# A four-layer network in float32 on one core: VectorE takes over two of eight weight subtractions in nine stages, and the ring of raw weight tiles goes from four slots to eight

## The chip, the core and the metric

The kernel runs on one core of one Trainium2 chip. The metric is device time in microseconds of one execution, median over runs. A core has TensorE (PE: matrix products into PSUM), VectorE (DVE), ScalarE (ACT), GpSimd (POOL) and SyncE (SP, which here issues the loads of the weights); each works through its own list of instructions in order and waits on semaphores for the others.

## The reference

One sequence of 256 tokens and 2048 channels runs through four layers: a gated linear attention with a linear recurrent unit, an mLSTM, a latent attention with a block attention, and a windowed attention with a dilated one, each with its norm, its gates, its input and output products. Nearly all of the arithmetic is in products of 256 tokens with float32 weight matrices. Cut down to the shape of one layer (the last):

```python
def odd_layer(x, mem, norm_g, w_in, sinks, mem_norm_g, w_mem_kv, w_out):
    h = rms_norm(x, norm_g) @ w_in
    qkv_c, qkv_d, q_mem, gate = split_cols(h, ODD_SPLITS)
    ...
    y = jnp.concatenate([o_c, o_d, o_m], axis=-1) * jax.nn.silu(gate)
    return x + (y @ w_out).astype(x.dtype)
```

## The kernel before

**Stages.** The weight products are 26 stages in a fixed order (`stage_table`): ein, ein_zx, ein_zb, ple0, eout, gate0, oqk, ogate, ov, ogz, ple1, oout, gate1, evc, evkpe, evmem, uq, ukv, evgate_a, evmoba, evgate_b, evout, odin, odmem, odgate, odout. A stage computes pairs: a pair is 2 output blocks of 128 channels by 256 tokens, and it is cut along the contraction into units, 8 for 16 blocks of the contraction and 10 for the 20 blocks of evout and the 18 of odout. A unit is a weight tile of 128 x 512 (four cells of 128 x 128; in odout the last two units of a pair have two cells). There are 1420 units in all, and every one is loaded once.

**A unit's way.** Float32 products are made of parts of fewer bits. For unit n: SP loads `raw` by DMA; ACT rounds it to `w_hi` (in `rounded`, line 738); POOL subtracts, `w_lo = raw - w_hi` (line 340); PE does three matmuls for each cell, `w_hi` with both halves of x and `w_lo` with the high half (lines 381 to 383). `raw`, `w_hi` and `w_lo` each have SLOTS = 4 slots. The waits between them are counts of units:

```python
sp.wait_ge(lo_ready, unit - SLOTS + 1)     # SP: load n after subtraction n - 4
act.wait_ge(unit_used, unit - SLOTS + 1)   # ACT: round n after PE used n - 4
pool.wait_ge(act_rounded, unit + 1)        # POOL: subtract n after rounding n
pe.wait_ge(lo_ready, st.unit0 + p * st.upp + q + 1)   # PE: use n after subtraction n
```

**What else the engines do.** DVE takes each finished pair out of PSUM (`take`, line 1217; in the output stages `hp + sums`, lines 1516 and 1837) and between two pairs does the work of the stage around: it splits activations into high and low halves (`split`, lines 1203 to 1207), adds squares for the next norm (`add_squares`, line 1257), multiplies h by the last gain (`gained`, line 1831), computes inverse roots (`root`, `inverse`, lines 1247 and 1270 to 1281) and rotates keys and queries (lines 1702 to 1705). In evout and odout (`add_out`) its body for pair p begins with the squares of pair p - 1:

```python
if not (isinstance(p, int) and p < 2):
    add(p - 1)                       # waits for ACT's square of pair p - 1
tt(hp, hp, sums_of(st, p, par), ADD).then_inc(pair_out, 1)
```

and ACT issues that square (line 777) right behind the rounding of unit 8 of pair p (`out_norm`, `q == 8`). In odin, pairs 0 to 5 also split a piece of the memory input (`memory`) behind `take`. PSUM banks alternate, so PE may be up to two pairs ahead of DVE.

`pairs_loop` makes two pairs one trip of a hardware loop where there are at least two trips.

Of the kernel before, what the change touches and what calls it, by code (L numbers as in the profile page):

```python
# [80 lines left out]

def stages():
# [26 lines left out]
def build(nc, A, out):  # L109
# [12 lines left out]
    with ctx:  # L122
# [58 lines left out]
        cols_loaded, consts_loaded = sem("cols_loaded"), sem("consts_loaded")  # L181
        unit_loaded = [sem(f"unit_loaded{i}") for i in range(SLOTS)]
        act_rounded, lo_ready, unit_used = sem("act_rounded"), sem("lo_ready"), sem("unit_used")
        pair_out = sem("pair_out")
# [84 lines left out]

        def pairs_loop(eng, count, body, first=0, steps=None, per=0):  # L270

            trips = (count - first) // 2
            if trips >= 2:
                n0 = steps.n if steps else 0
                with eng.Fori(0, trips) as i:  # L275
                    for k in range(2):
                        if steps:
                            steps.n = n0 + i * (2 * per) + k * per
                        body(i * 2 + (first + k), (first + k) % 2)
                if steps:  # L280
                    steps.n = n0 + trips * 2 * per
                first += 2 * trips
            for p in range(first, count):
                body(p, p % 2)

# [4 lines left out]
        def square_sums(name):  # L290
# [3 lines left out]
            return {"x2": (w[:, 40:42, :], 1), "ckv": (sq_next, 1)}.get(name, (sq_sum, 0))  # L294

        def unit_of(st, p, par, q):

            turn, slot = divmod(par * st.upp + q, SLOTS)
            loads = (p - par) * (st.upp * 16 // SLOTS) + (st.unit0 // SLOTS + turn + 1) * 16
            return slot, st.sizes[q], st.unit0 + p * st.upp + q, loads  # L300

# [3 lines left out]
        @block.sync  # L305
        def _(sp):
            def load(st):
                wd = A["w_" + st.name]

                def pair(p, par):  # L310
                    at = 0
                    for q in range(st.upp):
                        slot, n, unit, _ = unit_of(st, p, par, q)
# [7 lines left out]
                if st.unit0 == 0:  # L321
                    pair(0, 0)
                pairs_loop(sp, st.pairs, pair, first=int(st.unit0 == 0))

            for name in [r[0] for r in stage_table()]:
                load(ST[name])
            for k in range(4):
                sp.wait_ge(h_ready, HR["last"] + k + 1)
                sp.dma_start(out[:, 4 * k:4 * k + 4, :], h[:, 4 * k:4 * k + 4, :]).then_inc(out_stored, 16)
            sp.wait_ge(out_stored, 64)  # L330


        @block.gpsimd
        def _(pool):
            def split(st):
                def pair(p, par):
                    for q in range(st.upp):
                        slot, n, unit, _ = unit_of(st, p, par, q)
                        pool.wait_ge(act_rounded, unit + 1)  # L339
                        nc.gpsimd.tensor_tensor(w_lo[:, slot, 0:n], raw[:, slot, 0:n],  # L340
                                                w_hi[:, slot, 0:n].bitcast(F32), SUB).then_inc(lo_ready, 1)

                pairs_loop(pool, st.pairs, pair)

            for name in [r[0] for r in stage_table()]:
                split(ST[name])
# [3 lines left out]
        def _(pe):  # L350
            mm = nc.tensor.matmul

            def product(st, p, par, new=None, units=None):
# [9 lines left out]
                for q in units:  # L363
                    cells, slot = st.units[q], (par * st.upp + q) % SLOTS
# [21 lines left out]
            def products(name, first=0, count=None, new=None, behind=None, peel=1):  # L386


                st = ST[name]
                count = st.pairs if count is None else count  # L390

                def pair(p, par):
                    product(st, p, par, new if isinstance(p, int) and p == 0 else None)
                    if behind:
                        behind(p, par)

                for p in range(first, first + peel):
                    pair(p, p % 2)
                pairs_loop(pe, count, pair, first + peel)

# [312 lines left out]
        def _(act):  # L713
# [18 lines left out]
            def rounded(st, p, q, par=None):  # L732

                slot, n, unit, loads = unit_of(st, p, p % 2 if par is None else par, q)
                act.wait_ge(unit_loaded[slot], loads)
                if not (isinstance(p, int) and unit < SLOTS):
                    act.wait_ge(unit_used, unit - SLOTS + 1)
                af(w_hi[:, slot, 0:n], raw[:, slot, 0:n], ACT.Copy).then_inc(act_rounded, 1)  # L738

            def stage(name, first=0, count=None, peel=1, behind=None, done=0):  # L740
# [12 lines left out]
                for p in range(first, first + peel):  # L753
                    pair(p, p % 2)
                pairs_loop(act, count, pair, first + peel)

# [438 lines left out]
        def _(dve):  # L1195
# [4 lines left out]
            def split(src, gain, x, kt, count):  # L1200
# [7 lines left out]
                dve.wait_ge(x_ready, count)  # L1208

            def sums_of(st, p, par):  # L1210
# [8 lines left out]
            def store(name, buf, at, scale, first=0, count=None, adding=None, behind=0):  # L1219
# [10 lines left out]
                pairs_loop(dve, st.pairs if count is None else count, pair, first)  # L1230
                dve.wait_ge(pair_out, STORED[name] + (st.pairs if count is None else count))

# [97 lines left out]
            step(tt(col("ev_norm"), col("ev_norm"), col("final_norm"), MUL))  # L1330
            store("ein", w, 0, RS_LAYER, 3, 10, adding="mem", behind=2)
            store("ein", w, 0, RS_LAYER, 10, 11)
# [175 lines left out]
            def tail(l, x_out, x_h, x_next, gain_next, x_next_buf):  # L1508

                st = ST[f"ple{l}"]  # L1510
                pairs_loop(dve, 8, lambda p, par: take_plain(st, p, par), 4)
                so, xo = ST["eout" if l == 0 else "oout"], X[ST[f"gate{l}"].x]

                def out_pair(p, par):
                    hp = h[:, ds(p * 2, 2), :]
                    tt(hp, hp, sums_of(so, p, par), ADD).then_inc(pair_out, 1)  # L1516
                    dve.wait_ge(pair_out, so.pair0 + p + 1)
# [281 lines left out]
            def results_pair(name, rope_at, kind, nb, memory_behind=False):  # L1799
# [19 lines left out]
            def add_out(name, x_next, gain):  # L1819
# [13 lines left out]
                def pair(p, par):  # L1833
                    if not (isinstance(p, int) and p < 2):
                        add(p - 1)
                    hp = h[:, ds(p * 2, 2), :]
                    tt(hp, hp, sums_of(st, p, par), ADD).then_inc(pair_out, 1)  # L1837
# [10 lines left out]
                pairs_loop(dve, 8, pair, 2, steps=step, per=2 if x_next else 1)  # L1848
                add(7)
# [232 lines left out]
```

## Time and profile before

| | us |
|---|---|
| runs, median of 3 (lowest to highest) | 2476.62 (2474.54 to 2477.72) |
| the profiled execution | 2478.6 |
| its span, first to last instruction | 2476.8 |
| PE busy (share of the span) | 2290.4 (92%) |
| POOL busy | 1944.8 (79%) |
| DVE busy | 1319.7 (53%) |
| ACT busy | 1188.2 (48%) |

An instruction row gives start, length, engine, line, operation and tiles, and in brackets the idle time of the engine before it with what ended that. Matmul rows overlap: a matmul is shown for 0.28 us, and the next begins 0.12 us after it, so its pace is read from the starts. PEclk is the granted share of TensorE's 2.4 GHz: 1.00 is 2.4 GHz, 0.50 is 1.2 GHz.

### The profile page before, as it was taken

Reading aid. Unit: us, or ns where it says so; the run is one execution under the profiler, and the core shown is the slowest. Engines: PE = TensorE matmul, PEld = TensorE weight load, DVE = VectorE, ACT = ScalarE, POOL = GpSimd, SP = SyncE. Lnnn points to the kernel's source line nnn. Section 1 sums busy time; section 2 is a strip of 40 time slices with the busy share of each in tenths; the row PEclk is TensorE's granted clock in tenths of the full one; section 3 lists DMA queues with packets and bytes.
Section 4 is the critical chain, followed back from the end, with each engine's and each line's share of the span. In section 5 each row is a group of like instructions: output and inputs, shape, how many; then the busy total and the mean of one; then the engine's idle time right before and its main releaser. Section 6 shows DMA issues by size and latency. Waiting matters only on the chain.

```text
span 2476.8 us, 51508 instructions
## 1 busy us (share of the span) xinstructions
PE 2290.4 (92%) x17520; PEld 2189.3 (88%) x17520; DVE 1319.7 (53%) x1572; ACT 1188.2 (48%) x2068; POOL 1944.8 (79%) x1424
## 2 busy tenths in 40 slices
PE   6999876899997999989998899999999999998997
PEld 6998876899996799879987889999999999988997
DVE  6337686439607726764499654221743652058623
ACT  4454354444444445554443345444644444466643
POOL 5895566899987876669997965888679998855686
PEclk9999997999998999989999999999999999999998
DMA  6654332555554554435554543555456655533454
GB/s 204 193 170 136 103 102 77 161 183 158 169 174 137 174 174 132 124 119 173 179 152 147 151 135 119 167 170 165 131 163 185 180 180 173 181 120 117 127 170 149
DMA packets 211116, 379.27 MB, mean 153 GB/s; under 512 B 23440, under 2 KB 34320, under 8 KB 210832
## 3 DMA queue, kind: packets, MB, share of 16 engines
q1 hardware_dynamic: 205056, 363.95, 48.5%
q10 hardware_dynamic: 5904, 13.23, 1.6%
q8 instruction: 99, 1.62, 0.3%
q14 instruction: 57, 0.47, 0.1%
HBM read 374.99 MB, written 2.10 MB: 152 GB/s over the span
## 4 chain that ended last, share of the span: by engine, by line
POOL 47%; issue 34%; PE 11%; DVE 5%; POOLq 1%; DMA 0%; ACT 0%; DVEq 0%; SPq 0%; ACTq 0%
POOL w_lo L340 47%; PE ps L381 3%; PE ps L383 3%; PE ps L382 3%; POOLq L339 1%; DVE tb L1203 1%; DVE h L1535 1%; DVE tb L1534 1%; DVE sq L1257 0%; DVE xa L1207 0%; DVE w L1257 0%; DVE w L1530 0%; DVE w L1529 0%; POOLq L275 0%; DVE rs L1270 0%
## 5 line engine op out<-in xcount | busy, mean ns | idle before, releaser
L340 POOL TENSOR_TENSOR w_lo<-raw,w_hi 128x512 fp32r<-128x512 f32 (+1 forms) x1420 | 1944.6, 1393 | 513.6 <-ACT w_hi L738 478.2
L738 ACT ACTIVATE w_hi<-raw 128x512 fp32r<-128x512 f32 (+1 forms) x1420 | 857.3, 619 | 955.6 <-PE ps L383 412.5
L381 PE MATMUL ps<-xa,w_hi 128*128 128x256 f32 x2960 | 864.5, 292 | 69.3 <-POOL w_lo L340 31.9
L382 PE MATMUL ps<-xa,w_hi 128*128 128x256 f32 x2960 | 842.1, 284 | 0.0
L383 PE MATMUL ps<-xa,w_lo 128*128 128x256 f32 x2960 | 841.4, 284 | 0.0
L381 PEld LDWEIGHTS ps<-xa,w_hi 128*128 128x128 f32 x2960 | 571.6, 193 | 95.6 <-POOL w_lo L340 38.3
L381 PE MATMUL ps<-xb,w_hi 128*128 128x256 f32 x2160 | 625.7, 290 | 18.3 <-POOL w_lo L340 17.0
L382 PE MATMUL ps<-xb,w_hi 128*128 128x256 f32 x2160 | 612.1, 283 | 0.0
L383 PE MATMUL ps<-xb,w_lo 128*128 128x256 f32 x2160 | 611.8, 283 | 0.0
L382 PEld LDWEIGHTS ps<-xa,w_hi 128*128 128x128 f32 x2960 | 572.7, 193 | 1.0
L383 PEld LDWEIGHTS ps<-xa,w_lo 128*128 128x128 f32 x2960 | 572.2, 193 | 0.0
L381 PEld LDWEIGHTS ps<-xb,w_hi 128*128 128x128 f32 x2160 | 414.7, 192 | 36.2 <-POOL w_lo L340 26.9
L382 PEld LDWEIGHTS ps<-xb,w_hi 128*128 128x128 f32 x2160 | 415.1, 192 | 0.5
L383 PEld LDWEIGHTS ps<-xb,w_lo 128*128 128x128 f32 x2160 | 415.0, 192 | 0.0
L1217 DVE TENSOR_TENSOR w<-ps,rs 128x512 f32 (+2 forms) x89 | 61.0, 686 | 477.1 <-PE ps L383 474.8
L1257 DVE TENSOR_TENSOR sq<-sq 128x512 f32<-128x512 f32 x36 | 47.8, 1326 | 74.5 <-ACT sq L777 72.3
L381 PE MATMUL ps<-xs,w_hi 128*128 128x256 f32 x144 | 47.4, 329 | 30.9 <-DVE w L1235 14.7
L1516 DVE TENSOR_TENSOR h<-h,ps 128x512 f32 (+1 forms) x16 | 11.0, 688 | 111.9 <-PE ps L383 111.9
L373 PE MATMUL ps<-w_hi,xb 128*128 128x512 f32 x128 | 53.2, 415 | 16.9 <-POOL w_lo L340 16.8
L381 PEld LDWEIGHTS ps<-xs,w_hi 128*128 128x128 f32 x144 | 32.5, 226 | 32.9 <-issue 21.1
L1207 DVE TENSOR_TENSOR xb<-tb,xb 128x512 fp32r<-128x512 f32 (+1 forms) x43 | 52.1, 1212 | 2.6
L1837 DVE TENSOR_TENSOR h<-h,ps 128x512 f32 (+1 forms) x16 | 11.0, 688 | 79.3 <-PE ps L383 79.3
(291 smaller groups left out, 2302.8 us busy)
## 6 DMA issues: line engine op xcount, KB each, us to landing
raw<-w_gate_dram SPq DMA_DIRECT2D x128, 256.0 KB, 2.8
raw<-w_ogz_dram SPq DMA_DIRECT2D x128, 256.0 KB, 3.0
raw<-w_odin_dram SPq DMA_DIRECT2D x128, 256.0 KB, 3.0
raw<-w_evmoba_dram SPq DMA_DIRECT2D x112, 256.0 KB, 3.1
raw<-w_ein_dram SPq DMA_DIRECT2D x96, 256.0 KB, 3.1
raw<-w_evout_dram SPq DMA_DIRECT2D x80, 256.0 KB, 2.9
raw<-w_odgate_dram SPq DMA_DIRECT2D x72, 256.0 KB, 3.0
raw<-w_ein_zx_dram SPq DMA_DIRECT2D x64, 256.0 KB, 3.0
```

The costliest lines, as they stand in the source:

```text
L339: pool.wait_ge(act_rounded, unit + 1)
L340: nc.gpsimd.tensor_tensor(w_lo[:, slot, 0:n], raw[:, slot, 0:n], w_hi[:, slot, 0:n].bitcast(F32), SUB).then_inc(lo_ready, 1)
L373: mm(to, high, w_hi[:, slot, 0:st.width], start=(k == 0), stop=False)
L381: mm(to, w_hi[:, slot, at], x[:, x0 + k, 0:T], start=(k == 0), stop=False)
L382: mm(to, w_hi[:, slot, at], x[:, x0 + k, T:2 * T], start=False, stop=False)
L383: ins = mm(to, w_lo[:, slot, at], x[:, x0 + k, 0:T], start=False, stop=(k == st.blocks - 1))
L738: af(w_hi[:, slot, 0:n], raw[:, slot, 0:n], ACT.Copy).then_inc(act_rounded, 1)
L1203: step(tt(tb[:, :, :], src, wide(gain, 2), MUL))
L1207: tt(x[:, ds(kt, 2), T:2 * T], src, hi.bitcast(F32), SUB).then_inc(x_ready, 1)
L1217: tt(dst, sums_of(st, p, par), along(rs[:, scale, :], st.nb), MUL).then_inc(pair_out, 1)
L1257: tt(acc, acc, w[:, 42:44, :] if second else sq_next, ADD).then_inc(sq_added, 1)
L1534: step(tt(tb[:, :, :], gs[:, par, :, :], pl, MUL))
```

## The change

A table `LO_DVE` names nine stages. In each, from pair `lo_from` on, the subtraction of two units of every pair is done by DVE and no longer by POOL. DVE does them in a new function `lower`, which stands ahead of the pair's `take` in its list. The one count `lo_ready` becomes two, `lo_pool` and `lo_dve`, and `wait_lo` picks the one that a unit belongs to. `raw` gets RAW_SLOTS = 8 slots (`w_hi` and `w_lo` keep four), so SP loads unit n after the subtraction of unit n - 8. Loops turn by 2 pairs where a stage has a multiple of 4 units, else by 4; pairs below `lo_from` are written out, and with ten units a pair evout and odout are written out whole. One allocation for DMA descriptors is made smaller to make room.

```diff
+RAW_SLOTS = 8
+LO_DVE = {
+    "ein": (4, (3, 7)), "eout": (2, (4, 7)), "oqk": (2, (3, 7)), "oout": (2, (4, 7)), "evmoba": (1, (3, 7)),
+    "evout": (2, (5, 9)), "odin": (1, (3, 7)), "odmem": (0, (3, 7)), "odout": (2, (5, 9)),
+}
...
-        raw = sb("raw", [P, SLOTS, CELLS_MAX * P])
+        raw = sb("raw", [P, RAW_SLOTS, CELLS_MAX * P])
...
-                        if not (isinstance(p, int) and unit < SLOTS):
-                            sp.wait_ge(lo_ready, unit - SLOTS + 1)
+                        if not (isinstance(p, int) and unit < RAW_SLOTS):
+                            wait_lo(sp, st, p, q, RAW_SLOTS)
...
+                        if (not isinstance(p, int) or p >= st.lo_from) and q in st.lo_dve:
+                            continue
...
-                    pe.wait_ge(lo_ready, st.unit0 + p * st.upp + q + 1)
+                    wait_lo(pe, st, p, q)
...
+            def lower(st, p, par):
+
+                if isinstance(p, int) and p < st.lo_from:
+                    return
+                assert isinstance(p, int) or loop_first[0] >= st.lo_from or not st.lo_dve
+                for q in st.lo_dve:
+                    at, slot, n, unit, _ = unit_of(st, p, par, q)
+                    dve.wait_ge(act_rounded, unit + 1)
+                    tt(w_lo[:, slot, 0:n], raw[:, at, 0:n], w_hi[:, slot, 0:n].bitcast(F32), SUB).then_inc(lo_dve, 1)
...
                     dst = buf[:, ds(p * st.nb + at, st.nb), :]
+                    lower(st, p, par)
                     take(st, p, par, dst, scale)
...
                 def pair(p, par):
                     if not (isinstance(p, int) and p < 2):
                         add(p - 1)
+                    lower(st, p, par)
                     hp = h[:, ds(p * 2, 2), :]
```

How it stands in the lists at three places. First DVE in odout, one middle pair; `sq<-sq` is `add_squares`, `h<-h,cols` is `gained`, `h<-h,ps` takes the pair. Before:

```order
L1257 TENSOR_TENSOR sq<-sq 128x512 [waits sq_ready]
L1258 REGISTER_ALU
L1831 ISA [waits sq_added]
L1831 TENSOR_TENSOR h<-h,cols 128x512
L1212 ISA
L1837 ISA [waits unit_used]
L1837 TENSOR_TENSOR h<-h,ps 128x512
```

And in the changed kernel:

```order
L1322 TENSOR_TENSOR sq<-sq 128x512 [waits sq_ready,pair_out]
L1899 TENSOR_TENSOR h<-h,cols 128x512 [waits sq_added]
L1268 TENSOR_TENSOR w_lo<-raw,w_hi 128x512 [waits act_rounded]
L1268 TENSOR_TENSOR w_lo<-raw,w_hi 128x256 [waits act_rounded]
L1906 TENSOR_TENSOR h<-h,ps 128x512 [waits unit_used]
```

The subtractions of units 5 and 9 of the pair stand behind the square's addition and the gain, and ahead of the taking of the pair.

Second PE in odout at unit 5 of a pair. Before (the start of a unit in the loop):

```order
L383 MATMUL ps<-xb,w_lo 128x256
L367 REGISTER_ALU
L381 MATMUL ps<-xb,w_hi 128x256 [waits lo_ready]
L382 MATMUL ps<-xb,w_hi 128x256
L383 MATMUL ps<-xb,w_lo 128x256
```

In the changed kernel, from the last cell of unit 4 on:

```order
L430 MATMUL ps<-xb,w_hi 128x256
L431 MATMUL ps<-xb,w_hi 128x256
L432 MATMUL ps<-xb,w_lo 128x256
L430 MATMUL ps<-xb,w_hi 128x256 [waits lo_dve]
L431 MATMUL ps<-xb,w_hi 128x256
L432 MATMUL ps<-xb,w_lo 128x256
```

The number of matmuls is the same; the first one of unit 5 waits for DVE's count.

Third DVE at the start of odin, from the last step of the inverse root over pair 0 (its `take` and the memory piece) into the loop from pair 1. Before:

```order
L1281 TENSOR_TENSOR rs<-rs,tb 128x256 [waits dve_step]
L1217 TENSOR_TENSOR w<-ps,rs 128x512 [waits unit_used,rope_loaded,dve_step]
L1203 TENSOR_TENSOR tb<-sm,cols 128x512 [waits stream_loaded0]
L1206 CAST xb<-tb 128x2x256 [waits dve_step]
L1207 TENSOR_TENSOR xb<-tb,xb 128x2x256 [waits dve_step]
L275 UNCONDITIONAL_BRANCH [waits x_ready]
L275 ISA
L1217 ISA [waits unit_used]
L1217 TENSOR_TENSOR w<-ps,rs 128x512
```

In the changed kernel:

```order
L1346 TENSOR_TENSOR rs<-rs,tb 128x256 [waits dve_step]
L1277 TENSOR_TENSOR w<-ps,rs 128x512 [waits unit_used,rope_loaded,dve_step]
L1253 TENSOR_TENSOR tb<-sm,cols 128x512 [waits stream_loaded0]
L1256 CAST xb<-tb 128x2x256 [waits dve_step]
L1257 TENSOR_TENSOR xb<-tb,xb 128x2x256 [waits dve_step]
L292 UNCONDITIONAL_BRANCH [waits x_ready]
L292 ISA
L1268 TENSOR_TENSOR w_lo<-raw,w_hi 128x512 [waits act_rounded]
L1267 REGISTER_ALU
L1268 TENSOR_TENSOR w_lo<-raw,w_hi 128x512 [waits act_rounded]
L1277 ISA [waits unit_used]
L1277 TENSOR_TENSOR w<-ps,rs 128x512
```

The two subtractions of pair 1 stand behind the root, the taking of pair 0 and its memory piece.

## Rows read from the trace of the kernel before

**Rows 1.** The page: the chain that ended last, shares of the span by engine.

```profile
POOL 47%; issue 34%; PE 11%; DVE 5%; POOLq 1%; DMA 0%; ACT 0%; DVEq 0%; SPq 0%; ACTq 0%
```

**Rows 2.** Four pairs of oqk: us, busy us (instructions) of PE, PEld, DVE, ACT, POOL.

```profile
690.70:736.80 46.10, 46.10 (x386) 46.10 (x385) 2.79 (x5) 19.58 (x33) 40.15 (x33) 1.00 0.55 172
```

**Rows 3.** Waits of TensorE on POOL (us, times, longest): the span, ein, odout.

```profile
PE ps L381 <- POOL w_lo L340: 48.9, 55, 4.0
...
PE ps L381 <- POOL w_lo L340: 2.3, 3, 1.6
...
PE ps L381 <- POOL w_lo L340: 2.8, 7, 0.6
```

**Rows 4.** Timeline of evout pair 5: PE begins unit 5, ACT's unit 8 and square, DVE's addition.

```profile
1904.33 0.28 PE L381 MATMUL ps<-xb,w_hi 128*128 128x256 f32 x1
...
1904.56 0.64 ACT L738 ACTIVATE w_hi<-raw 128x512 fp32r<-128x512 f32 x1 [0.84 <-PE ps L383]
1905.10 0.62 ACT L777 ACTIVATE sq<-h 128x512 f32 x1
...
1905.75 0.69 DVE L1257 TENSOR_TENSOR sq<-sq 128x512 f32<-128x512 f32 x1 [3.57 <-ACT sq L777]
```

**Rows 5.** The same of odout pair 6, and DVE's gain.

```profile
2439.96 0.28 PE L381 MATMUL ps<-xb,w_hi 128*128 128x256 f32 x1
...
2439.91 1.10 ACT L738 ACTIVATE w_hi<-raw 128x512 fp32r<-128x512 f32 x2 [0.62 <-DMA raw<-w_odout_dram]
2440.91 0.62 ACT L777 ACTIVATE sq<-h 128x512 f32 x1
...
2441.57 0.90 DVE L1257 TENSOR_TENSOR sq<-sq 128x512 f32<-128x512 f32 x1 [7.79 <-ACT sq L777]
2442.74 0.87 DVE L1831 TENSOR_TENSOR h<-h,cols  x1 [0.28 <-DVE sq L1257]
```

**Rows 6.** Odin: DVE takes pair 0, ends its memory piece; PE begins unit 3 of pair 1.

```profile
1965.74 0.69 DVE L1217 TENSOR_TENSOR w<-ps,rs 128x512 f32<-128x512 f32 x1
...
1968.88 1.67 DVE L1207 TENSOR_TENSOR xb<-tb,xb 128x512 fp32r<-128x512 f32 x1
...
1959.35 0.28 PE L381 MATMUL ps<-xa,w_hi 128*128 128x256 f32 x1
```

**Rows 7.** DVE in odin from the taking of pair 3, first and last row; a split's step alone.

```profile
1991.86 0.69 DVE L1217 TENSOR_TENSOR w<-ps,rs 128x512 f32 x1 [3.39 <-PE ps L383]
...
1998.03 1.66 DVE L1705 TENSOR_TENSOR w<-w,tb 128x512 f32 x1
...
1950.38 0.69 DVE L1207 TENSOR_TENSOR xb<-tb,xb 128x512 fp32r<-128x512 f32 x1
```

**Rows 8.** Roots: ein pair 11 (DVE, PE begins unit 3), eout pair 2 (DVE, PE begins unit 4).

```profile
165.61 1.75 DVE L1270 RECIPROCAL rs<-rs 128x256 f32<-128x256 f32 x1 [4.83 <-ACT rs L797]
...
170.60 1.40 DVE L1281 TENSOR_TENSOR rs<-rs,tb 128x256 f32<-128x256 f32 x1
...
164.39 0.28 PE L381 MATMUL ps<-xa,w_hi 128*128 128x256 f32 x1
...
478.39 1.40 DVE L1281 TENSOR_TENSOR rs<-rs,tb 128x256 f32<-128x256 f32 x1
...
474.88 0.28 PE L381 MATMUL ps<-xb,w_hi 128*128 128x256 f32 x1
```

**Rows 9.** Stretches around two idle times of TensorE, columns as in Rows 2, then PEclk, DMA.

```profile
341.50:345.50 4.00, 0.01 (x1) 0.04 (x1) 3.82 (x7) 3.97 (x6) 1.48 (x2) 1.00 0.00 0
345.60:349.00 3.40, 3.40 (x15) 3.22 (x16) 3.29 (x4) 2.05 (x4) 3.40 (x3) 0.51 0.47 119
349.00:352.40 3.40, 3.40 (x25) 3.24 (x24) 3.37 (x2) 1.85 (x5) 1.94 (x2) 0.99 0.60 196
207.60:210.20 2.60, 0.01 (x1) 0.00 (x0) 2.54 (x5) 1.20 (x2) 0.00 (x0) 1.00 0.16 58
210.20:213.60 3.40, 3.38 (x29) 3.38 (x30) 1.22 (x1) 1.42 (x3) 2.95 (x3) 1.00 0.17 37
```

More of the change, by code:

```diff
@@ L80, in __init__, with by_dve @@
         self.unit0, self.pair0 = unit0, pair0
+        self.turn = 2 if self.upp % 4 == 0 else 4
+        self.lo_from, self.lo_dve = LO_DVE.get(self.name, (self.pairs, ()))
+    def by_dve(self, p, q):
+        return p >= self.lo_from and q in self.lo_dve
 def stages():
@@ L318, in pair @@
                         at += n
-                if st.unit0 == 0:
-                    pair(0, 0)
-                pairs_loop(sp, st.pairs, pair, first=int(st.unit0 == 0))
+                peel = min(st.pairs, (st.lo_from if st.lo_dve else 0) + -(-RAW_SLOTS // st.upp))
+                for p in range(peel):
+                    pair(p, p % st.turn)
+                pairs_loop(sp, st.pairs, pair, first=peel, turn=st.turn)
             for name in [r[0] for r in stage_table()]:
@@ L337, in pair @@
                     for q in range(st.upp):
-                        slot, n, unit, _ = unit_of(st, p, par, q)
+                        if (not isinstance(p, int) or p >= st.lo_from) and q in st.lo_dve:
+                            continue
+                        at, slot, n, unit, _ = unit_of(st, p, par, q)
                         pool.wait_ge(act_rounded, unit + 1)
-                        nc.gpsimd.tensor_tensor(w_lo[:, slot, 0:n], raw[:, slot, 0:n],
-                                                w_hi[:, slot, 0:n].bitcast(F32), SUB).then_inc(lo_ready, 1)
-                pairs_loop(pool, st.pairs, pair)
+                        nc.gpsimd.tensor_tensor(w_lo[:, slot, 0:n], raw[:, at, 0:n],
+                                                w_hi[:, slot, 0:n].bitcast(F32), SUB).then_inc(lo_pool, 1)
+                peel = st.lo_from if st.lo_dve else 0
+                for p in range(peel):
+                    pair(p, p % st.turn)
+                pairs_loop(pool, st.pairs, pair, first=peel, turn=st.turn)
             for name in [r[0] for r in stage_table()]:
@@ L395, in pair @@
                         behind(p, par)
+                peel = max(peel, min(count, st.lo_from) - first if st.lo_dve else 0)
                 for p in range(first, first + peel):
-                    pair(p, p % 2)
-                pairs_loop(pe, count, pair, first + peel)
+                    pair(p, p % st.turn)
+                pairs_loop(pe, count, pair, first + peel, turn=st.turn)
             def sums(name):
@@ L732, in rounded @@
             def rounded(st, p, q, par=None):
[L734 to L735 removed]
+                at, slot, n, unit, loads = unit_of(st, p, par, q)
+                act.wait_ge(unit_loaded[at], loads)
                 if not (isinstance(p, int) and unit < SLOTS):
                     act.wait_ge(unit_used, unit - SLOTS + 1)
[L738 removed]
+                af(w_hi[:, slot, 0:n], raw[:, at, 0:n], ACT.Copy).then_inc(act_rounded, 1)
             def stage(name, first=0, count=None, peel=1, behind=None, done=0):
@@ L753, in stage @@
                 for p in range(first, first + peel):
-                    pair(p, p % 2)
-                pairs_loop(act, count, pair, first + peel)
+                    pair(p, p % st.turn)
+                pairs_loop(act, count, pair, first + peel, turn=st.turn)
             def square(name, j, src, gain=None):
@@ L1228, in pair @@
                         add_squares(adding, p - behind)
-                pairs_loop(dve, st.pairs if count is None else count, pair, first)
-                dve.wait_ge(pair_out, STORED[name] + (st.pairs if count is None else count))
+                count = st.pairs if count is None else count
+                peel = max(first, min(count, st.lo_from)) if st.lo_dve else first
+                for p in range(first, peel):
+                    pair(p, p % st.turn)
+                pairs_loop(dve, count, pair, peel, turn=st.turn)
+                dve.wait_ge(pair_out, STORED[name] + count)
             def take_plain(st, p, par):
```

68 lines of the change are left out of this document (49 added, 19 removed).

## The prediction, made before the changed kernel ran

> **What bounds the kernel now.** I read the chain that ended last first: POOL has 47% of it and "issue" 34%, PE 11% [rows 1]. That looks as if the subtractions were the bound. Then I read a stretch of one of the nine stages, since a share over the span says nothing of them. In oqk four pairs, 32 units, take 46.1 us, 1.44 us a unit. A unit is 12 matmuls, and matmuls begin 0.12 us apart, so 12 x 0.12 = 1.44: TensorE is full and sets the pace, while POOL is busy for 40.15 us of the 46.1 (1.25 a unit) and has time left [rows 2]. PE's pace does not depend on the change; the number of matmuls and their clock stay. The chain names POOL because PE's issue is found to have been released by it, not because it is late. Third, the waits of PE on POOL, the only ones that an earlier low half can shorten: 48.9 us for the 256-column matmuls in the whole span, of which 2.3 in ein and 2.8 in odout; with 2.1 in eout, 1.6 in oout, 0.8 in evmoba, 1.9 in evout, 0.4 in odin and none in oqk and odmem the nine stages have 11.9 us [rows 3]. So what the change can give there is at most 12 us.
>
> **What it gives.** (1) In the nine stages DVE does 140 subtractions (16 in ein, 12 each in eout, oqk, oout, evout and odout, 26 in evmoba, 30 in odin, 8 in odmem) that POOL did. POOL gets free of them, but it wasn't the bound. Together with (2), eight raw slots, which let ACT round as soon as PE has freed a `w_hi` slot and not some 3 us after a subtraction, this may take away the 11.9 us. (3) In the other 17 stages PE's waits on POOL are 48.9 - 11.9 = 37.0 us, behind subtractions whose rounding is mostly late because ACT is at other work, which no slot of `raw` changes. I take 3 of them. Gain 15 us; bounds 5 and 22.
>
> **What it costs.** DVE works in order. A subtraction stands behind all that DVE does for the pair before, and PE cannot pass its unit without it. I ask in each stage when PE begins the unit and when DVE can be there. An operation of DVE on two tiles in SBUF takes 0.69 us alone (the last of [rows 7]) and up to 1.67 where it meets POOL [rows 6]; these are the bounds of one subtraction, and 0.7 to 1.0 is taken, since POOL stands still in most of these stalls (its next unit can't be rounded before PE goes on).
>
> (4) **evout, units 5 of pairs 2 to 7.** DVE's list has the square's addition ahead of the subtraction of unit 5. ACT issues that square behind its rounding of unit 8, which waits until PE has used unit 4. So the chain starts only when PE has finished unit 4: in pair 5 PE begins unit 5 at 1904.33; ACT starts unit 8 at 1904.56, the square ends at 1905.72, DVE adds from 1905.75 [rows 4]. With 0.69 to 1.67 for the addition and the same for the subtraction unit 5 can begin between 1907.2 and 1909.1: PE stands for 2.9 to 4.8 us. I take 3.4, as the addition meets POOL's unit 8 and the subtraction meets nothing. Six pairs: 20.4 us. Nothing hides it, since PE has no other work in its list there.
>
> (5) **odout, units 5 of pairs 2 to 7.** The same, and the gain too. PE begins unit 5 at 2439.96 and has finished unit 4 at about 2440.15. Unit 8 has half the size; the square ends 0.94 us after that rounding's start (it started at 2440.59 for want of its DMA, and the square ended at 2441.53; eight slots take this want away). Then 0.90 + 0.10 for the addition, 0.87 + 0.1 for the gain [rows 5] and 0.7: 2440.15 + 0.94 + 1.0 + 0.97 + 0.7 = 2443.76, a stand of 3.8 us (3.3 to 5.0). Six pairs: 22.5 us.
>
> (6) **odin.** Unit 3 of pair 1 is wanted at 1959.35, but DVE is in the inverse root and is through with pair 0's memory piece at 1970.55 [rows 6]: 11.2 + 0.7 = 11.9 us if it goes as before. While PE stands POOL soon does too, and of DVE's seven last steps most lose the meeting with it (0.7 to 1.0 each): I take 7.8 us (bounds 7 and 12). For pairs 2 to 6 DVE has 7.8 us of work behind a `take` (1991.86 to 1999.69 [rows 7]); PE is at unit 3 after 0.9 us of rotation and 3 x 1.44, 5.1 us later. With the subtraction that is 7.8 + 0.7 - 5.1 = 3.4, up to 4.4 met by POOL, and 0.7 if all seven steps take their bare 0.69. I take 2.0, five times: 10 us.
>
> (7) **Roots in ein and the two output stages.** In ein pair 11 unit 3 is wanted at 164.39, the root ends at 172.0; alone its last three steps would take 1.3 us less 0.2, ending near 169.2, so 169.95 - 164.39 = 5.6 us (bounds 5.5 and 8.4). In eout pair 2 unit 4 is wanted at 474.88, the root ends at 479.79, near 477 without POOL: 2.9 us; oout is the same with 3.0 (bounds 2.8 and 6 each) [rows 8]. Pair 4 of ein follows DVE's small work on parameters: 2 us.
>
> (8) In the remaining pairs of evmoba, odin, eout, oout and ein the slack is 0.1 to 2.3 us (unit wanted less DVE free less 1.0), so they cost about 1.5 us together, 0 to 8.
>
> (9) **The clock.** Where PE did nothing for 4.0 us the granted clock in the next 3.4 us was 0.51, with 15 matmuls, and 25 in the 3.4 us after that: 10 x 0.12 = 1.2 us lost. After 2.6 us without work it stayed at 1.00 [rows 9]. The 12 stands of (4) and (5), odin's first and ein's last are 3.4 us or more: 14 x 1.2; four of 2 to 3 us count 0.7: together 20 us (0 to 35). 1.2 GHz is the lower of the two levels.
>
> **Sum.** Costs 20.4 + 22.5 + 7.8 + 10 + 5.6 + 5.9 + 2 + 1.5 + 20 = 95.7, gain 15: +81 us. The profiled execution took 2478.6, so 2559.6; it was 2.0 above the median of the runs, so **2558 us**.
>
> SP, ACT and POOL have no added work; SP's waits come four units earlier, and the DMAs of `raw` are as many as before. PE's added register steps stand between units as before, one each.
>
> **Rivals.** (A) *The forecast*, 0.72: PE stands at DVE's units, mostly where evout and odout add squares.
>
> (B) *Faster.* The stands don't add, because PE loses nothing at the unit where it waits: this needs DVE to reach the subtraction before PE is there. The mechanism is POOL's relief with the eight slots; the price is a gain of 15 to 22 us, 2476.6 - 19 = 2458. It decides if ACT's square of pair p - 1 is done before PE uses unit 4 of pair p; then (4) and (5) fall away. Against it: ACT's square started at 1905.10 behind a rounding released by PE [rows 4]. For it: POOL has 47% of the chain [rows 1]. The roots would still cost. 0.08.
>
> (C) *Stands, but no lower clock, and DVE fast without POOL*: all low bounds, 17.4 + 19.8 + 7 + 3.5 + 5.5 + 5.6 + 1 + 0 = 60 less 22: 2515. 0.08.
>
> (D) *The meeting of DVE and POOL at its worst.* Every subtraction comes behind one of POOL's (1.3 us) and takes 1.67: 28.8 + 30 + 12 + 22 + 8.4 + 12 + 3 + 8 + clock 30 = 154, less 10: 2620. For it: DVE's split steps in odin took 1.3 to 1.67 where POOL was busy. Against: POOL has no rounded unit while PE stands. 0.08. The Trainium skill, "SBUF — State Buffer", section "Who interferes with whom", has a rule that speaks against this change: a VectorE operation with two SBUF inputs contends with a GpSimd one that reads SBUF, and the second to issue blocks fully until the first is finished. The trace agrees as far as 0.69 against 1.67 us goes. By that rule the time comes near (D) where POOL is always at work, and near the forecast where it stands.
>
> (E) *Nothing measurable*: stands of a few us that the gain of 15 pays for, 2477. It would need (4) and (5) to be a fifth of what I work out. 0.04.
>
> **Numbers.** The likeliest is (A). The range is to hold 8 in 10: from (C)'s 2515 up to 2600, which leaves out (B), (E), the lower half of (C) and (D). A measurement of this kernel can tell about 0.2% (5 us) from no change. Faster 0.08, same 0.04, slower 0.88.
>
> **What the profile after would show.** Right: PE waits on DVE's `w_lo` (line 1268) of 70 us or more, six each in evout and odout of about 3.4 and 3.8 us, one of about 8 in odin and one of about 5.6 at the end of ein, and half clock behind them; PE's waits on POOL in the nine stages near 0; oqk at 1.44 us a unit as before; POOL's share of the span down by some 180 us of busy time. Wrong: PE waits on line 1268 of under 20 us in all (then (B) or (E)), or light pairs that go below 1.44 us a unit (then PE's pace was not the bound).

## The result, and the profile after

The changed kernel took 2571.02 us (median of 4 runs, 2569.28 to 2572.15) beside 2477.17 us of the kernel before. The ratio is 1.038, 95% interval 1.0362 to 1.0398. The change costs 93.9 us. The forecast was 2558 us, 81 us more than before; its range, from (C)'s 2515 to 2600, holds the time.

Three lines of the page of the changed kernel: busy time and share of the span by engine, the granted clock in 40 slices, and the shares of the chain that ended last:

```profile
PE 2329.0 (91%) x17520; PEld 2232.2 (87%) x17520; DVE 1407.6 (55%) x1712; ACT 1186.2 (46%) x2068; POOL 1750.3 (68%) x1284
...
PEclk9999988999999999989999999999988899999987
...
PE 39%; DVE 11%; issue 4%; POOL 3%; ACT 1%; DVEq 0%; DMA 0%; POOLq 0%; ACTq 0%
```

POOL's busy time is down by 194.5 us, from 1944.8, as 140 subtractions would have it. Its share of the chain that ended last fell from 47% [rows 1] to 3%. Both look like the cure of a bound, and the kernel is slower. Four pairs of oqk, as in [rows 2], say why, with the same columns (busy us of PE, PEld, DVE, ACT, POOL, then PEclk):

```profile
690.00:736.10 46.10, 46.10 (x387) 46.10 (x386) 7.93 (x12) 20.23 (x33) 31.09 (x25) 1.00 0.56 174
```

POOL works 31.1 us of the 46.1 and not 40.2, DVE 7.9 and not 2.8, and PE issues 387 matmuls as before (386): TensorE was full, and stays so.

What TensorE waits for, in the span (us, times, longest). The first row is new, the second answers to [rows 3]:

```profile
PE ps L430 <- DVE w_lo L1268: 77.0, 22, 7.7
...
PE ps L430 <- POOL w_lo L386: 26.0, 28, 4.0
```

And the first row by stage: evout, odout, odin, ein, eout, oout.

```profile
PE ps L430 <- DVE w_lo L1268: 20.4, 6, 3.4
...
PE ps L430 <- DVE w_lo L1268: 19.6, 6, 3.3
...
PE ps L430 <- DVE w_lo L1268: 22.8, 6, 7.7
...
PE ps L430 <- DVE w_lo L1268: 6.7, 2, 5.3
...
PE ps L430 <- DVE w_lo L1268: 3.8, 1, 3.8
...
PE ps L430 <- DVE w_lo L1268: 3.7, 1, 3.7
```

These six make 77.0 us: 22 stands, all where the forecast put them, and none in oqk, evmoba and odmem. One stand of evout, on the timelines of PE, ACT and DVE (start, length, in brackets the idle time before and what ended it), which answers to [rows 4]:

```profile
1902.71 0.28 PE L432 MATMUL ps<-xb,w_lo 128*128 128x256 f32 x1
1906.38 0.58 PE L430 MATMUL ps<-xb,w_hi 128*128 128x256 f32 x1 [3.40 <-DVE w_lo L1268]
...
1903.08 0.63 ACT L788 ACTIVATE w_hi<-raw 128x512 fp32r<-128x512 f32 x1 [0.80 <-PE ps L432]
1903.62 0.61 ACT L827 ACTIVATE sq<-h 128x512 f32<-128x512 f32 x1
...
1904.34 1.27 DVE L1322 TENSOR_TENSOR sq<-sq 128x512 f32<-128x512 f32 x1 [3.94 <-ACT sq L827]
1905.63 0.69 DVE L1268 TENSOR_TENSOR w_lo<-raw,w_hi 128x512 fp32r<-128x512 f32 x1
```

PE ends unit 4; that lets ACT round unit 8; ACT's square follows; DVE adds it; only then does DVE subtract for unit 5, and PE goes on. It is a ring of waits over three engines (PE, ACT, DVE, and PE again), and POOL isn't in it; POOL only makes DVE's addition longer (1.27 us here, 0.69 in [rows 4]).

A comparison by stage (from the rounding of its first unit to that of the next stage's) gives evout +32.9, odin +30.8, odout +26.6, oout +5.3, eout +5.2, ein +5.0, oqk +1.3, odmem 0 and evmoba -0.2 us, and the 17 other stages together -15.5: the profiled spans differ by 91.4 us.

### The profile page after: what moved, and what is told of

The parts are those of the page before. It is cut to its first block, busy times and chain, and to the rows that moved or that the text cites. A ratio compares the mean times of both kernels' runs of the same rounds, so it can differ in the third digit from the quotient of the medians.

```text
span 2568.2 us, 48576 instructions
## 1 busy us (share of the span) xinstructions
PE 2329.0 (91%) x17520; PEld 2232.2 (87%) x17520; DVE 1407.6 (55%) x1712; ACT 1186.2 (46%) x2068; POOL 1750.3 (68%) x1284
## 4 chain that ended last, share of the span: by engine, by line
PE 39%; DVE 11%; issue 4%; POOL 3%; ACT 1%; DVEq 0%; DMA 0%; POOLq 0%; ACTq 0%
PE ps L430 12%; PE ps L431 12%; PE ps L432 12%; POOL w_lo L386 3%; PE ps L678 1%; DVE tb L1253 1%; DVE sq L1322 1%; PE ps L700 1%; DVE w_lo L1268 1%; DVE xa L1257 1%; PE ps L654 1%; DVE h L1602 0%; DVE rs L1335 0%; DVE tb L1601 0%; DVE w L1322 0%
## 5 line engine op out<-in xcount | busy, mean ns | idle before, releaser
L386 POOL TENSOR_TENSOR w_lo<-raw,w_hi 128x512 fp32r<-128x512 f32 (+1 forms) x1280 | 1750.1, 1387 | 791.4 <-ACT w_hi L788 747.7
L430 PE MATMUL ps<-xa,w_hi 128*128 128x256 f32 x2960 | 873.2, 295 | 90.5 <-DVE w_lo L1268 33.2
L431 PE MATMUL ps<-xa,w_hi 128*128 128x256 f32 x2960 | 850.8, 287 | 0.0
L430 PE MATMUL ps<-xb,w_hi 128*128 128x256 f32 x2160 | 639.0, 296 | 57.7 <-DVE w_lo L1268 43.8
L430 PEld LDWEIGHTS ps<-xa,w_hi 128*128 128x128 f32 x2960 | 580.3, 196 | 114.4 <-DVE w_lo L1268 35.0
L431 PE MATMUL ps<-xb,w_hi 128*128 128x256 f32 x2160 | 624.5, 289 | 0.0
L432 PE MATMUL ps<-xb,w_lo 128*128 128x256 f32 x2160 | 624.1, 289 | 0.0
L431 PEld LDWEIGHTS ps<-xa,w_hi 128*128 128x128 f32 x2960 | 581.0, 196 | 1.1
L430 PEld LDWEIGHTS ps<-xb,w_hi 128*128 128x128 f32 x2160 | 428.5, 198 | 75.1 <-DVE w_lo L1268 46.4
L431 PEld LDWEIGHTS ps<-xb,w_hi 128*128 128x128 f32 x2160 | 428.7, 198 | 0.5
L432 PEld LDWEIGHTS ps<-xb,w_lo 128*128 128x128 f32 x2160 | 427.6, 198 | 0.0
L1268 DVE TENSOR_TENSOR w_lo<-raw,w_hi 128x512 fp32r<-128x512 f32 (+1 forms) x140 | 115.9, 829 | 259.4 <-ACT w_hi L788 252.5
L1277 DVE TENSOR_TENSOR w<-ps,rs 128x512 f32<-128x512 f32 (+2 forms) x89 | 60.9, 686 | 263.7 <-PE ps L432 262.9
L1906 DVE TENSOR_TENSOR h<-h,ps 128x512 f32<-128x512 f32 x16 | 11.0, 688 | 91.7 <-PE ps L432 91.7
```

What stands on the lines that cost most here:

```text
L386: nc.gpsimd.tensor_tensor(w_lo[:, slot, 0:n], raw[:, at, 0:n], w_hi[:, slot, 0:n].bitcast(F32), SUB).then_inc(lo_pool, 1)
L430: mm(to, w_hi[:, slot, at], x[:, x0 + k, 0:T], start=(k == 0), stop=False)
L431: mm(to, w_hi[:, slot, at], x[:, x0 + k, T:2 * T], start=False, stop=False)
L432: ins = mm(to, w_lo[:, slot, at], x[:, x0 + k, 0:T], start=False, stop=(k == st.blocks - 1))
L1268: tt(w_lo[:, slot, 0:n], raw[:, at, 0:n], w_hi[:, slot, 0:n].bitcast(F32), SUB).then_inc(lo_dve, 1)
L1277: tt(dst, sums_of(st, p, par), along(rs[:, scale, :], st.nb), MUL).then_inc(pair_out, 1)
```

## The experiments

"The ring" is the ring of eight raw slots. Diffs are against the changed kernel. Each ratio is against the kernel before in runs beside it (medians 2475.55 to 2476.09).

**One part alone: the ring.** The table is empty.

```diff
-LO_DVE = {
-    "ein": (4, (3, 7)), ...
+LO_DVE = {
 }
```

> The changed kernel with an empty table LO_DVE: POOL does all subtractions, and what is left of the change is the ring of eight raw slots. In the profile of the changed kernel seven stages became longer by 106.9 us together, and the others shorter by 15.5. Theory: the 15.5 come from the ring alone, since they lie in stages where DVE has no subtraction: 2477 - 15 = 2462 us (2458 to 2467), with the nine stages within 3 us of before in all. Rival 1 (the forecast's own split: most of the gain is POOL's relief in the nine stages): 2477 - 3 = 2474. Rival 2 (the gain elsewhere is work that was only shifted across a stage's border by the late stages): 2477, no change.

Measured 2450.32 us, ratio 0.9888 (0.9869 to 0.9907): 25.4 us faster than before, more than any of the three said. The nine stages became 11.1 us shorter in all (odout 5.2, evout 3.3; oqk 1.5 longer), the 17 others 16.0. So the change holds a gain of 25 us and, on top of it, a loss of 120.7 us by DVE's subtractions.

**The other part alone: DVE's subtractions with four raw slots.**

```diff
-RAW_SLOTS = 8
+RAW_SLOTS = 4
```

> The changed kernel with RAW_SLOTS = 4, so DVE's subtractions without the ring. Theory: the two parts add up, and it is 15 us above the changed kernel: 2571 + 15 = 2586 us (2580 to 2592), with the stands at line 1268 as they are. Rival: with eight slots SP is far ahead, with four a late subtraction of DVE also holds back the next loads (SP waits for unit n - 4, which PE's stand makes late), so the stands get longer by a DMA of 3 us each, some 18 of them: 2625.

Measured 2596.94 us, ratio 1.0474 (1.045 to 1.0498). Against the kernel before that is +121.2 us; with the ring it was 2571.02 - 2450.32 = +120.7. The two parts add up. My 2586 was off only because it took the ring for 15 us. The rival's 3 us for each stand aren't there: the 22 stands take 85.3 us in the span for 77.0, 22.1 in evout for 20.4.

**DVE's order in evout and odout.**

```diff
                 def pair(p, par):
+                    lower(st, p, par)
                     if not (isinstance(p, int) and p < 2):
                         add(p - 1)
-                    lower(st, p, par)
```

> One line moved: in evout and odout lower(st, p, par) stands ahead of add(p - 1). Theory (the forecast's step: the subtraction of unit 5 stands behind the addition of a square that ACT issues only behind its rounding of unit 8): all 12 stands there (6 x 3.4 and 6 x 3.26 us) and the half clock behind them go; evout falls from 150.0 to about 117 us and odout from 154.2 to about 127: 2571 - 60 = 2511 us (2506 to 2518). Rival 1 (the stands are there because DVE is late from its split and output work of pair p - 1, or since ACT rounds unit 5 late): nothing changes, 2571. Rival 2 (the stand only moves: DVE now waits for unit 9's rounding, adds the square late and takes the pair late, and PE waits for its bank): 2571 - 60 + 12 x 1.5 = 2529.

Measured 2505.54 us, ratio 1.0114 (1.0095 to 1.0133): 65.5 us less than the changed kernel by one moved line (half a microsecond below the theory's range). Evout takes 113.7 us, exactly what it takes with the ring alone, and odout 122.2 (122.4). All of the two stages' loss hung on this order. It also says what the 24 subtractions there are worth when they cost nothing: nothing.

**Other units for DVE.**

```diff
-    "evout": (2, (5, 9)), "odin": (1, (3, 7)), ... "odout": (2, (5, 9)),
+    "evout": (2, (6, 9)), "odin": (1, (6, 7)), ... "odout": (2, (7, 9)),
```

> Other units for DVE: evout 6 and 9, odout 7 and 9 (both had 5 and 9), odin 6 and 7 (had 3 and 7); same number of subtractions. Theory: DVE is ready at the same moment as before, PE comes to the unit 1.44 us later per unit, so a stand shrinks by that: evout 3.4 - 1.44 = 2.0 us, odout 3.26 - 2.88 = 0.4, odin's first 7.7 - 4.3 = 3.4 and its others (3.1 and 2.6) nil. Without half clock where the stand is 2.0 or less: evout 117 + 12 = 129 us, odout 127.6 + 2.4 = 130, odin 198 + 3.4 + 1.5 = 203; in all 2571 - 21 - 24 - 26 = 2500 us (2493 to 2512). Rival 1 (a stand belongs to the operation of DVE, a meeting with POOL or its issue, and follows it wherever it stands): 2571. Rival 2 (the clock falls as well behind a stand of 2.0 us, by the 2 us each that evout now shows): 2512.

Measured 2494.62 us, ratio 1.0068 (1.005 to 1.0087). Evout took 128.6 us, odout 126.1, odin 202.0. A stand of evout (its timeline of PE) and the stands of evout, odin and odout (waits):

```profile
1867.65 0.39 PE L437 MATMUL ps<-xb,w_hi 128*128 128x256 f32 x1 [1.98 <-DVE w_lo L1275]
...
PE ps L437 <- DVE w_lo L1275: 11.9, 6, 2.0
...
PE ps L437 <- DVE w_lo L1275: 4.3, 1, 4.3
...
PE ps L437 <- DVE w_lo L1275: 2.3, 6, 0.4
```

3.40 became 1.98 for one unit later, 3.3 became 0.4 for two: 1.44 us for each unit, as worked out. DVE comes when it comes; what a stand costs is decided by the unit that is put there. In odin the five later stands are gone, as the theory had it, and the first is 4.3 us, not 3.4, since two of DVE's steps ahead of it now run beside POOL's subtractions and take 1.74 and 1.37 us. It also bears on the clock: behind five of evout's six stands of 1.98 us it stayed at 1.00, and behind one, of the same length, it was 0.50 for 3.4 us with 16 matmuls. The stretch behind the stand shown (columns as above):

```profile
1869.00:1872.40 3.40, 3.40 (x30) 3.40 (x30) 0.00 (x0) 1.35 (x3) 2.11 (x2) 1.00 0.85 293
```

**108 subtractions where DVE has time.**

```diff
-    "ein": (4, (3, 7)), "eout": (2, (4, 7)), ... "oout": (2, (4, 7)),
+    "eout": (3, (4, 7)), ... "oout": (3, (4, 7)),
-    "odin": (1, (3, 7)),
+    "odin": (7, (3, 7)),
...
 (and the moved line of evout and odout; the loops of odin and of the output stages begin a pair later)
```

> 108 of the 140 subtractions stay on DVE, but only where the traces show DVE in time: lower stands ahead of the addition of squares in evout and odout, eout and oout begin with pair 3, odin with pair 7, ein has none; oqk, evmoba and odmem as in the change; the ring has eight slots. With the ring alone it was 2450 us. Theory: POOL's relief is worth nothing, since TensorE is full in these stages, and no stand is left: 2450 us (2446 to 2456). Rival 1: the relief has a value that the stands hid: 2440 or less. Rival 2: smaller stands are left in many pairs (the term of 1.5 us in the forecast, bounds 0 and 8): 2456 to 2462.

Measured 2448.63 us, ratio 0.9882 (0.9865 to 0.9898), beside 2450.32 for the ring alone: 1.7 us, within what these runs can tell. With 108 of 140 subtractions taken from POOL and no stand left, the relief is worth nothing that can be measured.

**The ring's gain: when the loads start.** All subtractions on POOL, eight slots, but SP waits as if there were four.

```diff
-                        if not (isinstance(p, int) and unit < RAW_SLOTS):
-                            wait_lo(sp, st, p, q, RAW_SLOTS)
+                        if not (isinstance(p, int) and unit < 4):
+                            wait_lo(sp, st, p, q, 4)
```

> POOL does all subtractions and raw has eight slots, but SP waits for subtraction n - 4 as in the kernel before, not n - 8. So the loads start as early as before, and all else of the ring is kept. Theory: the ring's 25 us come from loads that start earlier (in the kernel before ACT's roundings wait for a DMA of raw, with the ring alone none does): 2476 us (2470 to 2481). Rival: part of the 25 us comes from the rest (slots twice as far apart, loops of four pairs in stages with odd units, the smaller descriptor memory): 2455 to 2468.

Measured 2471.17 us, ratio 0.998 (0.9968 to 0.9992). Some 5 us of the 25 come from the rest (2 to 8 by the interval), which of its parts was not tried; 21 come from the earlier loads. The waits of ACT on DMAs show it. Three of their rows in the kernel before (there are 23 rows and 513.9 us in all):

```profile
ACT w_hi L738 <- DMA raw<-w_gate_dram: 84.0, 89, 1.9
...
ACT w_hi L738 <- DMA raw<-w_odout_dram: 50.3, 50, 2.7
ACT w_hi L738 <- DMA raw<-w_evout_dram: 47.5, 52, 2.9
```

With eight slots and SP at n - 4 it is 484.7 us, and with the ring these two rows are all that is left, 2.9 us:

```profile
ACT w_hi L786 <- DMA raw<-w_evmem_dram: 2.1, 2, 1.9
ACT w_hi L786 <- DMA raw<-w_ein_dram: 0.8, 1, 0.8
```

**Two slots more, not four.** The same two lines with 6 in place of 4.

> As the run with n - 4, but SP waits for subtraction n - 6. A load takes 2.8 to 3.1 us from issue to landing, two units of 1.44 us. Theory: what is hidden is one DMA, so two units earlier give nearly all of it: 2450 to 2455 us. Rival: each slot gives its share (ACT's stretches of other work are absorbed by depth, the deeper the better): half-way, 2463 us (2458 to 2468).

Measured 2446.4 us, ratio 0.9871 (0.9854 to 0.9887), not slower than eight and below the theory's range. ACT's waits for raw are 7.4 us. Two units of 1.44 us cover a load of 2.8 to 3.0 us, and depth beyond that brings nothing.

**Odin from pair 2 on.**

```diff
-    "odin": (1, (3, 7)),
+    "odin": (2, (3, 7)),
...
-            pairs_loop(dve, 5, results_pair("odin", OD_ROT, 0, 2, True), 1, steps=step, per=4)
+            results_pair("odin", OD_ROT, 0, 2, True)(1, 1)
+            pairs_loop(dve, 5, results_pair("odin", OD_ROT, 0, 2, True), 2, steps=step, per=4)
```

> The changed kernel with odin's DVE subtractions from pair 2 on, not from pair 1. Theory (the backlog: the inverse root and the memory pieces of pairs 0 and 1 keep DVE busy to about 1978 on the time of the kernel before, and PE wants pair 2's unit 3 at about 1971): pair 1's stand of 7.7 us goes, but pair 2's grows from 3.1 to about 7.5; net -3.3 us and up to 2 of half clock: 2571 - 4 = 2567 us (2564 to 2569). Rival (the 7.7 us belong to the root alone, and pair 2 keeps its 3.1): 2571 - 7.7 - 2 = 2561 us (2558 to 2563).

Measured 2564.93 us (four runs, 2552.92 to 2566.1), ratio 1.0339 (1.0309 to 1.0369). Pair 1 has no stand any more, and pair 2's grew from 3.11 to 5.63 us. DVE's list there, from the end of the root on:

```profile
2000.95 1.40 DVE L1353 TENSOR_TENSOR rs<-rs,tb 128x256 f32<-128x256 f32 x1
2002.38 0.69 DVE L1284 TENSOR_TENSOR w<-ps,rs 128x512 f32<-128x512 f32 x1
...
2006.24 0.69 DVE L1284 TENSOR_TENSOR w<-ps,rs 128x512 f32<-128x512 f32 x1
...
2012.87 0.69 DVE L1779 TENSOR_TENSOR w<-w,tb 128x512 f32<-128x512 f32 x1
2013.59 0.69 DVE L1275 TENSOR_TENSOR w_lo<-raw,w_hi 128x512 fp32r<-128x512 f32 x1
```

No idle time from the root's end to the subtraction: the backlog is handed on from pair to pair. The theory holds in kind: the stands show it, more surely than the time does. Its 7.5 us was too much; the whole net saving was 6.1 us, between the 4 of the theory and the 10 of the rival.

**What a stand costs beyond its length.** PE gets 24 more matmuls ahead of its wait at the 12 places of evout and odout.

```diff
+                    if st.name in ("evout", "odout") and q == 5 and p >= 2:
+                        pe.wait_ge(act_rounded, st.unit0 + p * st.upp + q + 1)
+                        for _ in range(24):
+                            k, ob = cells[0]
+                            mm(ps[:, bank, 0:T], w_hi[:, slot, 0:P], x[:, k, 0:T], start=False, stop=False)
                     wait_lo(pe, st, p, q)
```

> The changed kernel with 24 extra matmuls of PE ahead of its wait for unit 5, in pairs 2 to 7 of evout and odout (12 places). They multiply by w_hi of unit 5, which is there, and add into the pair's PSUM, so the sums of these pairs are other ones: the times are read, not the values. At full clock 24 matmuls are 2.9 us, less than the stands of 3.4 and 3.26 us, so PE waits only some 0.4 us and DVE's chain is untouched. Asked is what the 12 stands cost beyond their own length: against the ring alone evout is 36.3 us longer with 20.4 us of stands, odout 31.8 with 19.6, so 28.1 us beyond. Theory: that is the half clock behind each stand. With PE at work it stays at 1.00, and the time falls by most of it: evout 150 to 135, odout 154 to 142, in all 2571 - 27 = 2544 us (2540 to 2550). Rival: it is the refilling of the units behind (ACT, POOL and SP stood still too): 2571 us (2567 to 2575). Both by halves: 2557.

Measured 2543.12 us, ratio 1.0267 (1.0241 to 1.0294): 27.9 us less than the changed kernel, with 288 more matmuls. Evout falls from 150.0 to 135.8 us and odout from 154.2 to 143.9, 24.5 of the 28.1 us in question; 3.4 of the 27.9 lie in stages that the edit doesn't touch. PE still waits 0.55 us at each place of evout and 0.41 at each of odout, and the clock behind them is 1.00. So it is the clock, not the refilling. A stand of evout in the changed kernel and what follows (columns as in [rows 9]), then the two stretches behind the same place with the added matmuls:

```profile
1902.95:1906.36 3.41, 0.04 (x1) 0.00 (x0) 1.96 (x2) 1.15 (x2) 1.94 (x2) 0.81 0.01 5
1906.45:1909.85 3.40, 3.40 (x16) 3.40 (x17) 0.00 (x0) 0.44 (x1) 0.00 (x0) 0.50 0.71 227
1909.85:1913.25 3.40, 3.40 (x23) 3.40 (x23) 0.69 (x1) 0.82 (x2) 0.57 (x1) 0.70 0.51 161
...
1897.50:1900.90 3.40, 3.40 (x28) 3.40 (x29) 0.69 (x1) 0.85 (x2) 0.00 (x0) 1.00 0.69 222
1900.90:1904.30 3.40, 3.40 (x31) 3.40 (x30) 0.00 (x0) 1.68 (x3) 2.61 (x3) 1.00 0.67 195
```

16 and 23 matmuls where full clock has 30: (14 + 7) x 0.12 = 2.5 us lost. With the added matmuls it is at full clock in both stretches. In PE's busy share nothing of this shows: it reads 3.40 of 3.40 in each.

**Eight slots of w_hi too, all subtractions on POOL.** The changed lines beside the empty table (PE's three matmuls and POOL's and DVE's operands take `at` for `w_hi`, the first pair of ein is written out, and the descriptor memory is 128 in place of 1024):

```diff
-        w_hi = sb("w_hi", [P, SLOTS, CELLS_MAX * P], F32R)
+        w_hi = sb("w_hi", [P, RAW_SLOTS, CELLS_MAX * P], F32R)
...
-                if not (isinstance(p, int) and unit < SLOTS):
-                    act.wait_ge(unit_used, unit - SLOTS + 1)
+                if not (isinstance(p, int) and unit < RAW_SLOTS):
+                    act.wait_ge(unit_used, unit - RAW_SLOTS + 1)
...
                         pool.wait_ge(act_rounded, unit + 1)
+                        if not (isinstance(p, int) and unit < SLOTS):
+                            pool.wait_ge(unit_used, unit - SLOTS + 1)
```

> The ring alone (POOL does all subtractions), and w_hi has eight slots too; ACT waits for PE's unit n - 8, and POOL waits for unit n - 4 for its slot of w_lo. By the traces ACT's roundings that are late behind ACT's other work hold PE up by some 190 us in the ring's kernel, nearly all in the stages with attention, scans or gates. Theory: ACT comes to this other work up to four units earlier, and part of the lateness goes: 2450 - 40 = 2410 us (2390 to 2435). Rival: that work is itself released by PE or DVE, so ACT just waits longer ahead of it: 2450 us (2445 to 2455).

Measured 2434.02 us, ratio 0.9826 (0.981 to 0.9843), 16.3 us less than the ring alone and the fastest of all. The time is within the theory's range, the size between theory and rival. POOL waits less for ACT's roundings (314.1 us for 433.7), but PE's waits on POOL stayed (34.1 us for 29.8), and ACT waits for loads of raw again (110.4 us for 2.9): it may now round as far ahead as SP may load. What the smaller descriptor memory has in the 16.3 us was not tried.

**The same with all 140 subtractions on DVE.** The same lines, the table full, and `dve.wait_ge(unit_used, unit - SLOTS + 1)` in `lower`.

> The changed kernel (with all 140 subtractions on DVE) with the same eight slots of w_hi. Theory of the stands in evout and odout: DVE's addition waits for a square that ACT issues behind its rounding of unit 8, and that rounding waits for PE's unit 4 only since w_hi has four slots. With eight it waits for unit 0, so the square is early, and the 12 stands go without any line moved; those of odin, ein, eout and oout stay, as they are DVE's own backlog. So against the same kernel with POOL alone it is + 31 (odin) + 12 (eout, oout) + 6 (ein) = + 49 us, not + 121. Rival (the square is late for another reason, such as sq's own slot or ACT's load): + 121, as now.

Measured 2477.02 us, ratio 1.0003 (0.9993 to 1.0013): + 43.0 us against POOL alone, not + 121. No order of DVE's work was changed, yet the waits of PE on DVE's subtractions in evout are

```profile
PE ps L432 <- DVE w_lo L1271: 0.9, 1, 0.9
```

and in odout there are none. In the span 30.7 us are left (77.0 in the changed kernel), in 11 places, ten of them in ein, eout, oout and odin. DVE's addition no longer waits for a square:

```profile
1863.74 0.69 DVE L1259 TENSOR_TENSOR xa<-tb,xa 128x512 fp32r<-128x512 f32 x1
1864.47 0.69 DVE L1325 TENSOR_TENSOR sq<-sq 128x512 f32<-128x512 f32 x1
1865.19 1.67 DVE L1271 TENSOR_TENSOR w_lo<-raw,w_hi 128x512 fp32r<-128x512 f32 x1
```

So both ways out of the ring of waits work: another order on DVE, or a deeper ring of `w_hi` that takes PE's unit 4 out of it. With the latter the kernel is level with the one before, since the 43 us that the subtractions on DVE still cost (30.7 of them in stands, by DVE's own backlog but for 0.9) eat what the two rings bring (41.5).

## Why the prediction was right, and where it was off

| step of the forecast | forecast, us | measured, us |
|---|---|---|
| (4) evout, 6 stands | 20.4 | 20.4 |
| (5) odout, 6 stands | 22.5 | 19.6 |
| (6) odin, first stand | 7.8 | 7.7 |
| (6) odin, five others | 10 | 15.1 |
| (7) ein's root, eout and oout | 5.6, 5.9 | 5.3, 7.5 |
| (7) ein pair 4 | 2 | 1.4 |
| (8) small ones | 1.5 | 0 |
| (9) the clock (measured: all the rest of the loss) | 20 | 43.7 |
| gain | 15 | 25.4 |
| net | 80.7 | 95.3 |

The stands are 77.0 us for 75.7. The clock's row is what is left of the loss, 120.7 - 77.0. The net is of the runs beside the ring alone; in the first comparison it was 93.9.

**The bound (first part) was right for the nine stages.** "TensorE is full and sets the pace" in oqk is what the two rows show, and the run with 108 subtractions shows it for the time. The chain's 47% for POOL was not a bound.

**The mechanism of the stands was right.** One moved line gave back all of evout's and odout's loss, and a stand shrinks by 1.44 us for each unit that it is put later. Rival (B) named this very condition, "if ACT's square of pair p - 1 is done before PE uses unit 4 of pair p; then (4) and (5) fall away": the run with eight slots of `w_hi` makes it true, and the 12 stands fall away.

**(9), the clock, was mis-sized by a factor of two.** I took 10 matmuls lost from the difference of two stretches in [rows 9], 15 and 25. The measure is against full clock, 29 or 30 in such a stretch (the last row of [rows 9] has 29), and the second stretch isn't full either. Behind evout's stands it is 16 and 23; the loss is 2.65 us each ((36.3 - 20.4) / 6, evout's 150.0 against 113.7 with the ring), behind odout's 2.0 and behind odin's six, of 2.6 to 7.7 us, 1.4 in the mean. Where the second stretch is full the loss is less, as in odin behind the stand of pair 2:

```profile
2021.20:2024.60 3.40, 3.38 (x16) 3.38 (x17) 0.00 (x0) 0.41 (x1) 0.00 (x0) 0.51 0.62 183
2024.60:2028.00 3.40, 3.40 (x30) 3.40 (x30) 0.69 (x1) 1.49 (x3) 1.30 (x2) 1.00 0.79 268
```

The filled stands show that it is the clock for 24.5 of the 28.1 us there. For the other stages, 15.6 us of the 43.7, that is argued, not tried.

**(6), odin's middle pairs.** My own sum said 3.4 us (3.3 with 0.9 + 3 x 1.44 = 5.2 in place of its 5.1), and I took 2.0, between that and the 0.7 of seven bare steps. Each was 3.1 (the last 2.6). The first steps did run at 0.69 or less, but the last two (1.19 and 1.65 us) and the subtraction itself met POOL:

```profile
2015.12 0.69 DVE L1257 TENSOR_TENSOR xb<-tb,xb 128x512 f32 x1
...
2017.86 1.65 DVE L1772 TENSOR_TENSOR w<-w,tb 128x512 f32 x1
2019.63 1.54 DVE L1268 TENSOR_TENSOR w_lo<-raw,w_hi 128x512 fp32r<-128x512 f32 x1
...
2015.98 4.64 POOL L386 TENSOR_TENSOR w_lo<-raw,w_hi 128x512 fp32r<-128x512 f32 x3 [2.45 <-ACT w_hi L788]
```

**(5) and (7), the smaller errors.** Odout's stand was 3.26 us and not 3.8: from start to start the addition took 0.84 us for 1.0, the gain 0.61 for 0.97. Eout's was 3.85 and not 2.9: one step of the root still met POOL (1.37 us), and DVE stood 0.25 us ahead of the subtraction.

**The meeting of DVE and POOL (rival D).** The 140 subtractions took 829 ns in the mean, nearer to 0.69 than to 1.67. "POOL has no rounded unit while PE stands" held only in part. In each of the longer stands POOL was at work for 1.3 to 2.5 us; but in 16 of the 22 it was through when DVE's subtraction began, which took 0.69. In the six others (ein's pair 4, odin's pairs 2 to 6) the subtraction met it and took 1.2 to 1.5 us. The 108 in the repaired kernel, 862 ns in the mean, never stood in PE's way.

**The gain.** Its size was forecast at 15 and was 25, and the reasons were mixed up. Of the 11.9 us of PE's waits on POOL in the nine stages I said that POOL's relief, "together with" the slots, may take them away. With the ring alone 4.6 us of them are left and the nine stages are 11.1 us shorter; with 108 subtractions on DVE as well 4.6 are left again, so the relief added nothing. For the 17 other stages I took 3 us, as their waits lie behind late roundings "which no slot of `raw` changes", and they gave 16.0. That is the step of the forecast that was wrong: the slots do change it, and in the whole span these waits fell from 48.9 to 29.8 us. I had read only what PE waits for. The rows that would have told are ACT's waits for DMAs of `raw`, 513.9 us: a load began only after the subtraction four units back and took 2.8 to 3.1 us, so the roundings and subtractions behind it ran late. That this left no slack for ACT's stretches of other work, and so made PE wait, is argued and not tried by itself. The clock came out 23.7 us dearer than forecast and the gain 10.4 us larger. That these errors offset each other by nearly half, and the time is only 13 us off, is luck.

## What to carry to other kernels

Before work is moved to an engine that has time on average, ask for each moved operation when its result is wanted and what stands ahead of it in that engine's list, and follow that wait back: if it ends at the very engine that will wait, the operation closes a ring, and the price is paid in every pair. An engine that the chain names isn't the bound where the one behind it never lacks work; freeing it gave nothing here. And size a ring of buffers by the transfer that it must hide, here two more slots for one load, before asking which engine does the arithmetic.

## What the runs showed of the hardware

A stand of PE costs more than its length. After the stands of 3.1 to 3.4 us in evout, odin and odout the granted clock was 0.50 to 0.58 for 3.4 us (1.2 GHz for all or most of them), and the price on top, worked out by stage, was 1.4 to 2.65 us each. Length alone does not decide: after five of six stands of 1.98 us it stayed at 1.00, and after the sixth it was 0.50. A PE that was given matmuls of no use during the stand kept its clock, and the kernel became 27.9 us faster by doing more, 24.5 of them in the two stages with the added matmuls. I had expected a price of 1.2 us.
